# Fox attention in a two-block network: the dense panels of a head in pieces over its four turns, the gate panel with its own head

## What is computed

```python
def fox_attention(u, w_in, b_f, q_norm_g, k_norm_g, w_out):
    proj = u @ w_in
    q, k, v, g, fl = jnp.split(proj, [D_MODEL, 2 * D_MODEL, 3 * D_MODEL, 4 * D_MODEL], axis=-1)
    q = rms_norm(q.reshape(bn, sn, FOX_HEADS, FOX_HD), q_norm_g).transpose(0, 2, 1, 3) * (FOX_HD ** -0.5)
    k = rms_norm(k.reshape(bn, sn, FOX_HEADS, FOX_HD), k_norm_g).transpose(0, 2, 1, 3)
    v = v.reshape(bn, sn, FOX_HEADS, FOX_HD).transpose(0, 2, 1, 3)
    f_cum = jnp.cumsum(jax.nn.log_sigmoid(fl + b_f), axis=1).transpose(0, 2, 1)
    for blk in range(sn // FOX_BLOCK):        # blocks of 128 queries
        s = jnp.einsum('bhtd,bhsd->bhts', q[:, :, t0:t1], k[:, :, :t1])
        s = s + f_cum[:, :, t0:t1, None] - f_cum[:, :, None, :t1]
        p = jax.nn.softmax(jnp.where(mask, s, -jnp.inf), axis=-1)
        outs.append(jnp.einsum('bhts,bhsd->bhtd', p, v[:, :, :t1]))
    return (o * jax.nn.sigmoid(g)) @ w_out
```

## Time and profile before

| what | value |
|---|---|
| median of 3 runs | 2879.48 us (2876.84 to 2880.65) |
| the profiled execution | 2875.85 us, its span 2874.4 us |
| TensorE busy | 2709.7 us, 94% of the span |
| VectorE, ScalarE busy | 1639.1 us (57%), 1102.8 us (38%) |
| mean granted TensorE clock | 0.979 |
| share of PE in the chain that ended last | 47%, next ACT and DVE with 3% each |

### The profile page before, as it was taken

The page is one execution under the profiler, slowest core; times in us unless marked ns, Lnnn a source line. Parts: engine busy times, 40 slices in busy tenths (PEclk is TensorE's granted clock), DMA queues, the critical chain, the costliest instruction groups (busy, mean ns, idle before and its releaser), DMA issues.

```text
span 2874.4 us, 40281 instructions
## 1 busy us (share of the span) xinstructions
PE 2709.7 (94%) x16544; PEld 2153.1 (75%) x16544; DVE 1639.1 (57%) x2925; ACT 1102.8 (38%) x1900; POOL 9.4 (0%) x21
## 2 busy tenths in 40 slices
PE   5999999989998899998998899999989989999998
PEld 4776888867665688886876777888868767788886
DVE  6587646563555775667456665444455577533334
ACT  3544324234555442323344443222334354432223
POOL 0000000000000000000000000000000000000000
PEclk9999999999998999999999999999999999999999
DMA  6445555542221365663230013344433200232322
GB/s 250 139 150 165 195 172 183 168 140 79 69 67 46 101 203 193 190 201 120 103 118 16 3 46 123 133 153 146 141 112 102 97 3 2 74 103 95 100 95 85
DMA packets 92086, 336.31 MB, mean 117 GB/s; under 512 B 10480, under 2 KB 10736, under 8 KB 91776
## 3 DMA queue, kind: packets, MB, share of 16 engines
q1 hardware_dynamic: 86800, 315.40, 33.2%
q10 hardware_dynamic: 3792, 14.11, 1.4%
q0 software_dynamic: 1312, 4.23, 0.5%
HBM read 331.57 MB, written 2.13 MB: 116 GB/s over the span
## 4 chain that ended last, share of the span: by engine, by line
PE 47%; ACT 3%; DVE 3%; issue 1%; DMA 0%; DVEq 0%; ACTq 0%
PE bank L633 12%; PE bank L635 12%; PE bank L634 12%; PE bank L891 1%; PE bank L866 1%; PE bank L877 1%; PE bank L654 1%; ACT probs L2198 1%; PE bank L655 1%; PE bank L656 1%; PE bank L1143 1%; PE bank L968 1%; PE bank L1184 0%; PE bank L1133 0%; PE bank L1145 0%
## 5 line engine op out<-in xcount | busy, mean ns | idle before, releaser
L633 PE MATMUL bank<-in_high,weights_high 128*128 128x512 f32 x2032 | 806.6, 397 | 13.5 <-DVE in_low L1384 9.1
L635 PE MATMUL bank<-in_high,weights_low 128*128 128x512 f32 x2032 | 793.7, 391 | 0.0
L634 PE MATMUL bank<-in_low,weights_high 128*128 128x512 f32 x2032 | 793.5, 391 | 0.0
L1235 DVE TENSOR_TENSOR weights_low<-weight_ring,weights_high 128x1024 fp32r<-128x1024 f32 x404 | 493.8, 1224 | 426.3 <-ACT weights_high L1956 426.2
L1956 ACT ACTIVATE weights_high<-weight_ring 128x1024 fp32r<-128x1024 f32 x404 | 424.3, 1051 | 451.5 <-PE bank L635 301.9
L633 PEld LDWEIGHTS bank<-in_high,weights_high 128*128 128x128 f32 x2032 | 382.8, 188 | 120.0 <-issue 25.1
L634 PEld LDWEIGHTS bank<-in_low,weights_high 128*128 128x128 f32 x2032 | 383.0, 188 | 80.9 <-issue 3.6
L635 PEld LDWEIGHTS bank<-in_high,weights_low 128*128 128x128 f32 x2032 | 382.9, 188 | 81.0
L633 PE MATMUL bank<-hidden_split,weights_high 128*128 128x512 f32 x864 | 336.9, 390 | 0.0
L635 PE MATMUL bank<-hidden_split,weights_low 128*128 128x512 f32 x864 | 336.1, 389 | 0.0
L634 PE MATMUL bank<-hidden_split,weights_high 128*128 128x512 f32 x864 | 336.1, 389 | 0.0
(11 more groups left out here) (379 smaller groups left out, 2958.8 us busy)
## 6 DMA issues: line engine op xcount, KB each, us to landing
weight_ring<-stream SPq DMA_DIRECT2D x597, 512.0 KB, 3.5
mixer_out<-cmp ACTq DMA_DIRECT2D x6, 1024.0 KB, 4.8
hidden<-forget_rows POOLq DMA_DIRECT2D x16, 256.0 KB, 3.9
residual<-x ACTq DMA_DIRECT2D x4, 512.0 KB, 12.1
mixer_out<-cmp SPq DMA_DIRECT2D x2, 1024.0 KB, 6.5
out<-mixer_out ACTq DMA_DIRECT2D x4, 512.0 KB, 2.7
constants<-consts ACTq DMA_DIRECT2D x1, 1821.5 KB, 20.0
silu_c<-c ACTq DMA_DIRECT2D x2, 512.0 KB, 4.1
```

The source lines that it names most:

```text
L633: pe.matmul(bank[:, :], WHI[:, z, cols], high, start=(k == 0), stop=False)
L634: pe.matmul(bank[:, :], WHI[:, z, cols], low, start=False, stop=False)
L635: ins = pe.matmul(bank[:, :], WLO[:, z, cols], high, start=False, stop=(k == ktiles - 1))
L1235: v.tensor_tensor(WLO[:, z, :], ring[:, n % RING, :], WHI[:, z, :].bitcast(F32), ALU.subtract).then_inc(*mark("weights_low", "low", n))
```

## The change

The diff does five things:

- It reorders the stream: `fk` 0 ahead of the second value pass, and then, for each head, `fq` and `fk` of the next head and `fg` of the head itself.
- TensorE's prologue is `fq` 0, `fk` 0, values 1, with both first norms between the second and the third of the four value panels. `fg` 0 is no longer in the prologue.
- The `fill` of TensorE issues pieces, given by `FOX_FILL`: turn r=0 has k-tiles 0 to 6 of `fq` (21 matmuls), r=1 the last of `fq` and 0 to 3 of `fk` (15), r=2 k-tiles 4 to 7 of `fk` (12), r=3 the whole `fg` of the current head (24). The norms stay in r=1 and r=2. In the last head's four turns `fg` 7 is issued, 6 matmuls in each.
- ScalarE's and VectorE's `fill` follow: `raw` of the queries moves from turn 0 to 1, of the keys from 1 to 2, `gate` from 2 to 3, and the splits to turns 0, 1 and 3.
- In the last head ScalarE waits (`fox_input_free`) until a piece of `fg` 7 has read the input tiles that it then overwrites, and one split stands ahead of that.

```diff
-    keys += [("fl",)] + [("fv", 0, n) for n in range(4)] + [("fq", 0)] + [("fv", 1, n) for n in range(4)]
-    keys += [("fk", 0), ("fg", 0)] + [(n, hp) for hp in range(1, KT) for n in ("fq", "fk", "fg")]
+    keys += [("fl",)] + [("fv", 0, n) for n in range(4)] + [("fq", 0), ("fk", 0)] + [("fv", 1, n) for n in range(4)]
+    for hp in range(KT):
+        keys += [("fq", hp + 1), ("fk", hp + 1), ("fg", hp)] if hp < KT - 1 else [("fg", hp)]
...
+    FOX_FILL = ((("fq", 0, 0, 7),), (("fq", 0, 7, 8), ("fk", 0, 0, 4)), (("fk", 0, 4, 8),), (("fg", -1, 0, 8),))
...
+        def gemm_some(key, a, b):
+            bank = gemm_bank(key) if a == 0 else B_of(key)
+            n, = PANELS[key]
+            z = split_turn[n] % NSPLIT
+            if a == 0:
+                pe.wait_ge(*at("low", n))
+            for j in range(a, b):
+                cols = slice(j * P, j * P + P)
+                high, low = u_split(j)
+                pe.matmul(bank[:, :], WHI[:, z, cols], high, start=(j == 0), stop=False)
+                pe.matmul(bank[:, :], WHI[:, z, cols], low, start=False, stop=False)
+                ins = pe.matmul(bank[:, :], WLO[:, z, cols], high, start=False, stop=(j == KT - 1))
+            if b == KT:
+                ins.then_inc(*mark("panels_used", "used", n))
+                ev.also("panels_used", "gemm", key)
+            return ins
...
             gemm(("fq", 0), u_split)
+            gemm(("fk", 0), u_split)
             pe.wait_ge(*at("fv_out", 0, NTB - 1))
-            gemm_tok(("fv", 1), 4, 2, 512, ("fv", 1), B[4:8])
-            norm(0, 0)
-            gemm(("fk", 0), u_split)
-            gemm(("fg", 0), u_split)
-            norm(0, 1)
+            gemm_tok(("fv", 1), 4, 2, 512, ("fv", 1), B[4:8], first_norms)
...
-                if part == 0 and r < 3:
-                    gemm((("fq", "fk", "fg")[r], hp), u_split)
-                if part == 1 and r in (1, 2):
+                if part == 0 and hp < KT:
+                    for name, of, a, b in FOX_FILL[r]:
+                        gemm_some((name, hp + of), a, b)
+                if part == 0 and hp == KT:
+                    ins = gemm_some(("fg", KT - 1), 2 * r, 2 * r + 2)
+                    if r < 3:
+                        ins.then_inc(*mark("tensor_fox", "fox_input_free", r))
+                if part == 1 and r in (1, 2) and hp < KT:
                     norm(hp, r - 1)
...
-                    if part == 0 and r < 3:
-                        prepare(ahead((("fq", "fk", "fg")[r], hp)))
+                    if part == 0 and r != 2:
+                        prepare(ahead((("fq", hp), ("fk", hp), None, ("fg", hp - 1))[r]))
...
+                elif part == 0 and r == 0:
+                    prepare(ahead(("fg", KT - 1)))
...
             raw(0, 0)
+            raw(0, 1)
+            prepare(ahead(("fv", 1, 1)))
+            root(0, 0)
+            root(0, 1)
             evict_blocks(("fv", 1), ("fv", 1, 3), B[4:8], lambda b: H[:, 13 + 2 * b, :], 512, ("fv_out", 1))
-            root(0, 0)
-            raw(0, 1)
-            gate(0)
-            root(0, 1)
...
+                if part == 0 and r == 3 and hp <= KT:
+                    gate(hp - 1)
                 if hp < KT:
                     if part == 0:
-                        if r < 2:
-                            raw(hp, r)
+                        if r == 0:
+                            prepare(ahead(("fq", hp)))
+                        elif r == 1:
+                            raw(hp, 0)
+                            prepare(ahead(("fk", hp)))
                         elif r == 2:
-                            gate(hp)
+                            raw(hp, 1)
...
                 elif hp == KT and part == 0 and r < 3:
+                    if r == 0:
+                        prepare(ahead(("fg", KT - 1)))
+                    s.wait_ge(*at("fox_input_free", r))
```

More of the change, by code:

```diff
@@ L659, in gemm_pair, with gemm_tok @@
                         ev.also("panels_used", "gemm", keys[used.index(n)])
-        def gemm_tok(name, panels, per, width, event, banks):
+        def gemm_tok(name, panels, per, width, event, banks, between=lambda i: None):
             for i in range(panels):
+                between(i)
                 n, = PANELS[(*name, i)]
@@ L902, in norm, with first_norms @@
                 ins.then_inc(*mark("tensor_fox", "fox_mean", hp, z))
+            def first_norms(i):
+                if i == 2:
+                    norm(0, 0)
+                    norm(0, 1)
             gemm(("fq", 0), u_split)
+            gemm(("fk", 0), u_split)
             pe.wait_ge(*at("fv_out", 0, NTB - 1))
-            gemm_tok(("fv", 1), 4, 2, 512, ("fv", 1), B[4:8])
-            norm(0, 0)
-            gemm(("fk", 0), u_split)
-            gemm(("fg", 0), u_split)
-            norm(0, 1)
+            gemm_tok(("fv", 1), 4, 2, 512, ("fv", 1), B[4:8], first_norms)
             def begin(d):
@@ L918, in fill @@
                 hp, r = d // 4 + 1, d % 4
-                if hp >= KT:
-                    return
-                if part == 0 and r < 3:
-                    gemm((("fq", "fk", "fg")[r], hp), u_split)
-                if part == 1 and r in (1, 2):
+                if part == 0 and hp < KT:
[6 more added lines that the diff above has]
+                if part == 1 and r in (1, 2) and hp < KT:
                     norm(hp, r - 1)
@@ L1625, in fox @@
             prepare(ahead(("fq", 0)))
+            prepare(ahead(("fk", 0)))
+            prepare(ahead(("fv", 1, 1)))
+            normed(0, 0)
+            normed(0, 1)
             prepare(ahead(("fv", 1, 3)))
[L1627 to L1630, removed]
             def bias(i):
```

## The result

| | before | after |
|---|---|---|
| median | 2880.07 us (2876.84 to 2881.66, 4 runs) | 2859.66 us (2857.75 to 2861.07, 4 runs) |
| profiled execution, span | 2875.85 us, 2874.4 us | 2857.75 us, 2856.3 us |
| mean granted clock | 0.979 | 0.985 |

The ratio of the runs is 0.9929, 95% interval 0.9918 to 0.9941: 20.4 us faster, between 17 and 24. I had said 2863.6 us, 15.9 us faster, with a range of 2856 to 2872.

A forecast was written before the change was run, and what follows sets the result against it. TensorE, busy for 94% of the span, was taken as the bound, so only its idle time and clock loss could be gained. Terms -8.6 - 9.9 + 2.6 = -15.9 us moved the median from 2879.5 to 2863.6 us, range 2856 to 2872.

The forecast's parts named there:

- The prologue: Ahead of the first scores: fg 0 leaves (5.44 us) and the 3.17 us wait goes; -8.6 us in all.
- Turns 0 to 27: The seven heads: -14.3 waits, -6.3 clock, +9.6 new waits, +0.7 bank changes make -10.3; the layout's -9.9 us was taken.
- The waits in turn 3: Seven heads: 24 matmuls ahead of the product remove its 2.04 us wait; 14.3 us gained.
- rival D: The 2.04 us wait moves elsewhere in turn 3 or 0, say behind gate; 2877.9 us; chance 0.05.
- The new wait: Turn r=2, ahead of the keys' norm: 7.67 us chain against 6.3 of work; 1.4 us, first head 1.0; 9.6 together.
- The clock: Four of seven heads lose 1.5 to 1.6 us to a low clock after turn 3's wait; 6.3 us gained.
- The last head: Turns after the seven heads: fg 7's 24 matmuls, a split and gate add +2.6 us; bounds +1.8 and +4.7.
- The pieces: Last head: four pieces of fg 7, 1.4 us each; 3.7 us hidden in product waits, 1.8 left.
- Gate and split: Last head: split (1.04 us) and gate (1.9) ahead of ScalarE's steps; at most 2.9 us more, at least nothing.
- Rival A: New waits in turn r=2 bring the clock down in all seven heads, 11.2 us lost; 2874.8 us; chance 0.12.
- Rival B: Turn r=2's new wait does not appear, ScalarE reading keys out earlier; gain 9.6 us larger, 2854.0 us; chance 0.08.
- Rival C: Turns 1 and 2 keep 8.5 and 8.9 us, set by ScalarE and VectorE; 2885.3 us, slower; chance 0.05.

The follow-up runs named there:

- e2: Kernel before with the new prologue alone, fg 0 still in it and the turns as before; 2874.62 us, ratio 0.9983 to before.
- e3: Kernel before plus 8 matmuls nobody reads in turn 3 of each head but the last; 2869.12 us, ratio 0.9963 to before.
- e8: Changed kernel with six fk matmuls moved from turn 2 to turn 1 (21, 21, 6, 24); 2877.97 us, ratio 0.9998 to before.
- e1: Kernel before run once more, nothing changed; 2879.04 us, ratio 0.9998; its profiled execution took 2874.99 us.
- e5: Changed kernel with 15, 15, 18 and 24 matmuls in turns 0 to 3 in place of 21, 15, 12, 24; 2852.76 us, ratio 0.9909 to before.
- e4: Changed kernel with the heads' panels undivided: 24, 24, 0 and 24 matmuls in turns 0 to 3; 2893.83 us, ratio 1.0052 to before.
- e10: Changed kernel with only the last head's gate moved behind ScalarE's copy in turn 31; 2851.57 us in one run, last head 23.29 us.
- e6: Changed kernel with last head's gate behind turn 31's copy and second output panel's split in turns 32 and 33; 2855.94 us, ratio 0.9924 to before.
- e9: Changed kernel with the division of e5 and the last-head order of e6 together; 2848.37 us, ratio 0.9901 to before.

## Why the prediction was right, and where it was not

**The prologue**, -8.6: measured -8.68. Its parts are the wait, 3.24 (e2), and the panel, 5.44.

**Turns 0 to 27**, -9.9: measured -10.66 against the profile that the sum was made on. The waits in turn 3 went, and nothing came at the product behind `gate` (rival D is out: no wait at L898 in turns 3 or 0). The new wait came where I put it and for the reason given. Its chain, forecast at 7.67, took 7.66. Its length was 1.1 and not 1.4 us, since TensorE's own work between the norms is longer: the idle time of a row is counted from the modelled end of the last small matmul, 0.15 us behind the pace at which these start, and a piece costs a little more than its matmuls. The head came to 28.8 us, as I had it (28.9). Turn 1 was covered.

The working gave back 9.6 us for seven new waits, where its own lengths (six of 1.4 and one of 1.0) make 9.4; the waits measured 7.3. The number taken, -9.9, is that of the layout and not of the sum.

**The clock.** The mechanism is shown as far as turn 3 goes: e3 fills the wait, and the falls are gone with heads otherwise as long. e8 brings falls back with a longer wait of the changed kernel. The price of a fall, 1.5 to 1.6 us, is right. The count is not: the prediction reads four falls behind the seven waits, and there are five, the last of them just behind the seventh head and so in the next stage. And the number changes: turns 0 to 27 have four falls in the first profile and six in e1.

**What was missed**, 4.5 us: the sum said -15.9 and the medians moved by 20.4. Of this the stages between the two profiled executions hold 1.4 (0.8 of it in turns 0 to 27, 0.6 in the last head), and the stretches outside the attention 0.8. The other 2.3 us are what the medians moved more than the profiled executions. It is likely that falls of the clock have a part in them: with e1's turns in place of the first profile's the stages sum to -8.68 - (213.68 - 199.92) + 2.02 = -20.4 us, and e3's runs too gained 10.4 us where its stages have 6.7 against the first profile and 9.9 against e1. It is not shown, since no profile was taken of an execution of before near the median. I had noted that the median lay 3.6 us above the profiled execution and carried the gain over unchanged. A fast execution is not simply one with few falls in the attention either: that of e1 has six in its turns and lies 4 us under its median.

**The last head**, +2.6 with bounds 1.8 and 4.7: measured +2.02. The number is near by luck, and three terms of its working were wrong. The pieces were charged with 1.8 us and cost nothing. Gate and split were charged with 0 to 2.9 us and cost 0.95 + 2.08 = 3.0, the split more than its own length on ScalarE. And the fall ahead of this stage, 0.95 us, was not in the sum; with turn 3's wait it went. Together 3.0 - 0.95 = 2.1. This stage goes by the chain of VectorE and ScalarE; TensorE's pieces lay beside it.

**Rival A**, the new waits cost clock too, did not come: all heads at 1.00. Its argument "in only four of seven heads" should read five. e8 shows that it had its point, only not with waits of 1.1 us. The rule of the Trainium skill ("TensorE: Matmul & The Clock Gate", "Part 4: PE-mode transpose"), that transposes don't count as a busy PE in the same way, is not decided here: the same transposes stood around waits of 1.1 and of 2.1 us in the seven heads, and only the latter saw the clock fall. **Rival B** did not come in the change; e5 made it, by cover and not by an earlier readout. **Rival C** did not come: turns 1 and 2 took 6.73 and 7.62 us, together 14.4, where it would have had 17.4.

## What to carry to other kernels

Where TensorE is busy for 94%, look for the turn whose wait recurs, lay out the chain between two of its instructions step by step, and give that turn as many matmuls as the chain is longer than the work; six matmuls in the right or the wrong turn were 7 us gained and 18 us lost. Count a recurring wait at more than its length if the clock falls behind it, and take the number of falls from more than one execution. When a step moves onto the queue of an engine that sets the pace of a stretch, lay it out on each engine that it touches: here one such step cost half of its length (the gate, beside a copy of VectorE that was nearly as late) and another the lengths of both its halves (the split). Matmuls moved into such a stretch cost nothing here. And before a difference of two stages is put down to an edit, look whether the clock was the same in both.

## What the hardware did that I had not expected

- 56 matmuls whose results nobody reads made the kernel 10.4 us faster (e3). They were put where TensorE would have waited 2.04 us, seven times.
- The clock's answer to a recurring wait of the seven heads changes much within a us: after 1.1 us no fall in 24 heads; after 2.04 us a fall in five and in six of seven (before, e1); after 2.14, with 0.26 at the product before it, in four of six (e8). With waits of 1.85 and of 1.86 to 2.14 us close together each head from the second on was at 0.90 (e4). That two executions of one program differ in which heads are hit was new to me as well.
- Among the small matmuls of the last head it is less orderly. A wait of 2.4 us in turn 29 was followed by a fall in after, e5 and e8 and by none in e4 and e10. A wait of 1.19 us at the product of turn 30 saw the clock fall in e6 and e9, where the same wait (1.18) in e10 did not.

```profile
897.60:900.80 3.20, 2.36 (x14) 1.36 (x14) 1.27 (x3) 2.81 (x6) 0.00 (x0) 0.52 0.00 0
```

The row is e6, from the last third of that wait on.
